# The level-1 block of a triangular inverse: masked from PSUM, or from a copy in SBUF

## The reference, cut to what matters

```
def step(s, inp):                      # s: one 64x64 state per head and direction
    r_t, w_t, k_t, v_t, aa_t, bb_t = inp
    sa = einsum('dbhij,dbhj->dbhi', s, aa_t)
    s = s * w_t[..., None, :] + sa[..., :, None] * bb_t[..., None, :] + v_t[..., :, None] * k_t[..., None, :]
    y_t = einsum('dbhij,dbhj->dbhi', s, r_t)
    return s, y_t
state, ys = lax.scan(step, state0, xs)  # 256 context tokens, then 256 latent tokens, 2 directions, 8 heads
```

## Time and profile before

| what | value |
|---|---|
| median of 3 runs | 2276.77 us (2275.12 to 2277.88) |
| profiled execution | 2275.12 us, its span 2273.3 us |
| PE busy | 2195.0 us, 97% of the span |
| DVE busy | 691.6 us, 30% |
| ACT busy | 355.3 us, 16% |
| POOL busy | 96.9 us, 4% |
| mean granted PE clock | 0.989 of full speed |

### The profile page before, as it was taken

How to read it: one execution, slowest core, us unless ns; L and a number is a source line. 1 busy time by engine, 2 the same in 40 slices (tenths; PEclk the granted TensorE clock), 3 DMA queues, 4 the chain that set the end, 5 groups by cost and what they waited for, 6 DMA issues and landing times.

```text
span 2273.3 us, 34037 instructions
## 1 busy us (share of the span) xinstructions
PE 2195.0 (97%) x15007; PEld 1350.1 (59%) x15008; DVE 691.6 (30%) x1187; ACT 355.3 (16%) x771; POOL 96.9 (4%) x114
## 2 busy tenths in 40 slices
PE   7999999999999998999998999999999999999997
PEld 6667786888677775478887553344344444444432
DVE  0000100621275424347777531211111211211113
ACT  1000200240100012243343111000001110100000
POOL 1000000000100000202212000000000000000000
PEclk9999999999999999999999989999999999999999
DMA  9655444244678961000001589999999999999996
GB/s 318 189 155 184 170 139 148 84 139 152 213 250 275 285 213 56 1 3 3 3 22 50 210 344 426 425 426 423 426 424 427 426 422 419 421 424 426 426 426 273
DMA packets 199428, 582.16 MB, mean 256 GB/s; under 512 B 9620, under 2 KB 153808, under 8 KB 166384
## 3 DMA queue, kind: packets, MB, share of 16 engines
q1 hardware_dynamic: 194656, 564.70, 64.4%
q0 software_dynamic: 4208, 13.27, 1.6%
q10 hardware_dynamic: 416, 1.99, 0.2%
HBM read 576.52 MB, written 3.42 MB: 255 GB/s over the span
## 4 chain that ended last, share of the span: by engine, by line
PE 91%; DVE 5%; DMA 2%; ACT 1%; issue 1%; SPq 1%; DVEq 0%
PE ps L2581 22%; PE ps L610 13%; PE ps L2593 10%; PE ps L671 8%; PE ps L619 7%; PE ps L1340 5%; PE ps L2560 3%; PE ps L2608 3%; PE ps L802 2%; PE ps L775 2%; PE ps L1670 2%; PE ps L1690 1%; PE ps L1772 1%; PE ps L976 1%; DMA arena<-in_w 1%; PE ps L1687 1%
## 5 line engine op out<-in xcount | busy, mean ns | idle before, releaser
L2581 PE MATMUL ps<-ring,const 128*64 128x512 f32 (+1 forms) x1536 | 474.5, 597 | 0.0
L2581 PEld LDWEIGHTS ps<-ring,const 128*64 128x64 f32 (+1 forms) x1536 | 160.8, 144 | 306.5 <-issue 306.2
L610 PE MATMUL ps<-arena,ring 128*128 128x256 f32 x1408 | 314.1, 381 | 1.8 <-DMA ring<-in_ffn_w_down 1.8
L610 PEld LDWEIGHTS ps<-arena,ring 128*128 128x128 f32 x1408 | 265.2, 190 | 46.5 <-issue 11.0
L2581 PE MATMUL ps<-arena,const 128*64 128x512 f32 (+1 forms) x512 | 225.7, 593 | 0.0
L2593 PE MATMUL ps<-ring,const 128*64 128x512 f32 (+1 forms) x768 | 190.1, 594 | 0.0
L671 PE MATMUL ps<-arena,ring 128*128 128x256 f32 x800 | 173.1, 379 | 0.0
L2805 DVE TENSOR_SCALAR arena<-ps 128x1024 f32<-128x1024 f32 x18 | 22.0, 1225 | 469.2 <-PE ps L2581 469.2
L671 PEld LDWEIGHTS ps<-arena,ring 128*128 128x128 f32 x800 | 151.9, 190 | 20.7
L619 PE MATMUL ps<-ring,arena 128*128 128x512 f32 x352 | 157.6, 592 | 0.0
L2593 PEld LDWEIGHTS ps<-ring,const 128*64 128x64 f32 (+1 forms) x768 | 65.1, 143 | 111.7 <-issue 110.2
(11 more groups left out here) (484 smaller groups left out, 2400.8 us busy)
## 6 DMA issues: line engine op xcount, KB each, us to landing
ring<-in_w SPq DMA_DIRECT2D x96, 2048.0 KB, 17.7
ring<-in_w SPq DMA_DIRECT2D x96, 1024.0 KB, 15.2
arena<-in_w SPq DMA_DIRECT2D x32, 2048.0 KB, 18.6
ring<-in_w_in SPq DMA_DIRECT2D x26, 1536.0 KB, 6.9
arena<-in_w SPq DMA_DIRECT2D x32, 1024.0 KB, 17.5
ring<-in_w_ada SPq DMA_DIRECT2D x16, 1536.0 KB, 9.2
ring<-in_ffn_w_gate SPq DMA_DIRECT2D x44, 512.0 KB, 3.9
ring<-in_ffn_w_up SPq DMA_DIRECT2D x44, 512.0 KB, 5.4
```

What stands on the lines that cost most here:

```text
L610: ins = pe.matmul(ps[:, j % 2, half * S:(half + 1) * S], s[:, col0:col0 + P], uT[:, k, :], start=(k == 0), stop=(k == KD - 1))
L2581: ins = pe.matmul(ps[a * n:(a + 1) * n, q, :], xsT[:, k, a * n:(a + 1) * n], chunk(chunks[a])[:, q * 512:(q + 1) * 512], start=False, stop ...
```

## The change

DVE no longer takes `near` out of PSUM. The 2x2 blocks for `TI[:, 1]` are now taken from `MbT`, which the first two mask instructions have just written to SBUF, under a mask `lev1` that is built like those of the other levels. This instruction stands behind `first` instead of ahead of it. PE's second products wait for the two `Mb` counts instead of `near`. POOL's wait for `T0` at the second level is gone. The constant table loses two masks of 64 columns and gains one.

```
@@ -145,8 +145,7 @@
         after = (ic > jc) if d == 0 else (ic < jc)
         cols[f"first{d}"] = after & ((ic // 2) == (jc // 2))
-        cols[f"near{d}"] = before & ((ic // 2) == (jc // 2))
-    for b in (2, 4, 8, 16, 32):
+    for b in (1, 2, 4, 8, 16, 32):
         cols[f"lev{b}"] = ((ic // (2 * b)) == (jc // (2 * b))) & ((ic // b) != (jc // b))
@@ -1642,7 +1641,7 @@
         def products_end_pe(pe, v):
-            pe.wait_ge(*at("near", v + 1))
+            pe.wait_ge(*at("Mb", 2 * v + 2))
             with_rows(pe, v, KT).then_inc(*up("Mk_mm"))
@@ -1974,8 +1973,6 @@
                     if n >= 2:
                         p.wait_ge(*at("Z_mm", 2 * (n - 1)))
-                    if l == 1:
-                        p.wait_ge(*at("T0", v + 1))
                     p.tensor_tensor(ME[:, (n % 2) * RH:(n % 2 + 1) * RH, :], MbT[v % 2][:, 0, :, :],
@@ -2024,6 +2021,7 @@
+            every = [P, RH, HN]
@@ -2031,13 +2029,11 @@
             for b in range(2):
                 masked(MbT[q], b).then_inc(*up("Mb"))
-            def inner(dst, b, name):
-                return d.tensor_tensor(dst.rearrange("p (b q) n -> p b q n", b=2), halves(b, 0).rearrange("p b (q n) -> p b q n", n=HN),
-                                k_(name).unsqueeze(1).unsqueeze(1).to_broadcast([P, 2, HP, HN]), ALU.mult)
-            inner(TI[q][:, 1, :, :], 0, f"near{dr}").then_inc(*up("near"))
             d.wait_ge(*at("Ti_mm", v + 1))
-            inner(TI[q][:, 0, :, :], 2, f"first{dr}").then_inc(*up("dve_own"))
-            d.wait_ge(*now("near"))
+            d.tensor_tensor(TI[q][:, 0, :, :].rearrange("p (b q) n -> p b q n", b=2), halves(2, 0).rearrange("p b (q n) -> p b q n", n=HN),
+                            k_(f"first{dr}").unsqueeze(1).unsqueeze(1).to_broadcast([P, 2, HP, HN]), ALU.mult).then_inc(*up("dve_own"))
+            d.wait_ge(*now("Mb"))
+            d.tensor_tensor(TI[q][:, 1, :, :], MbT[q][:, 0, :, :], k_("lev1").unsqueeze(1).to_broadcast(every), ALU.mult).then_inc(*up("dve_own"))
             d.wait_ge(*now("dve_own"))
             d.tensor_tensor(TI[q], TI[q], id64.unsqueeze(1).unsqueeze(1).to_broadcast([P, 2, RH, HN]), ALU.add).then_inc(*up("T0"))
```

## The result

The changed kernel takes **2297.08 us** (median of 6 runs, 2293.89 to 2299.93), the kernel before 2276.66 us (6 runs): ratio 1.0094, 95% interval 1.0084 to 1.0103. It is 20.4 us slower. The direction was forecast, the size was not: the forecast was 12.8 us, and 2297.08 lies above the range, which ended at 2294.0.

A forecast was written before the change was run, and what follows sets the result against it. PE was taken as the bound, busy 97% of the span, with DVE mattering where PE waits for `T0`. Late `T0`, 8 x 1.60 = 12.8 us, on the 2276.77 us median gave 2289.6 us; range 2283.5 to 2294.0.

The forecast's parts named there:

- `T0` on the path in all 8 visits: PE before L1670: any delay of `T0` delays the end equally, 8 times; bringing it forward gains at most 4.9 us.
- L2036 ends 0.55 after POOL, POOL 1.13 after it, the addition 1.09 after that; 1.60 a visit: DVE meeting POOL's level masks: these three delays make `T0` 1.60 us late per visit, 12.8 us in all.
- The alternation: DVE and POOL take turns by whole instructions, so POOL's second mask goes ahead of the identity addition; 1.60 us a visit.
- the addition goes first: Rival: the identity addition on DVE runs ahead of POOL's second mask; 0.71 us a visit, 2282.5 us; chance 0.05.
- So the visits bear such gaps: PE before L1670: idle may grow from 0.5 to 2.1 us, about 3.1 in visit 7, without the clock falling.
- the rival of the clock: PE's clock falls behind the longer gaps: 1.2 us a visit, 9.6 in all, on top; about 2299 us; chance 0.03.
- The row at 0.70 in the same group: Earlier trace, stretch 1262 to 1266: granted clock 0.70 with PE busy 2.57 of 4 us; basis for the clock rival's price.
- visit 7 as the first: By the skill's rule on idle gaps, visit 7, with the longest gap, would be first to lose PE's higher clock.
- Everything hidden: Side effects on PE, POOL and DVE hidden behind other waits, each taken as worth 0.
- PE's earlier second products: They may start 0.6 us earlier, when `Mb` is complete; worth 0, at most 0.6 us.
- POOL's earlier second mask: Ready about 1.4 us before PE could use it, its result not needed until the second level; worth 0.
- the order on DVE: `first` stands where `near` stood, five instructions of the same widths before `T0`; taken as 0, at most 0.1 us a visit.

The follow-up runs named there:

- The run with the gap filled: The changed kernel with two useless 512-column matmuls behind PE's second products in each visit; 2290.80 us, ratio 1.0059 to the kernel before.
- POOL's freedom alone: The kernel before without POOL's wait for `T0` at the second level, `near` still from PSUM; 2280.44 us, ratio 1.0011.

## Why the prediction was wrong

- **`T0` on the path in all 8 visits**: right. There were 18.1 us of waits against 17 to 18 forecast.
- **L2036 ends 0.55 after POOL, POOL 1.13 after it, the addition 1.09 after that; 1.60 a visit**: right: 0.54, 1.13, 1.08, and 1.58 in visit 1. The run with the gap filled measures the whole term: 13.5 us where 12.8 were forecast.
- **The alternation**: right for this kernel, but read too widely. It is not that a waiting POOL goes ahead of any DVE instruction. Who is queued at the moment of release goes. The rival "the addition goes first" had its real condition there, 0.05 us away.
- **The step that failed** is "So the visits bear such gaps", in the rival of the clock. It got 0.03 and was the case. It rested on two stretches of the earlier trace rows with a clock of 1.00 and little work on PE. One holds a single wait of 2.58 us, the other two, of 1.56 and 0.92, all in one execution. The runs show in its place that the clock may or may not fall behind a gap of one length, as in visits 1 and 2 of the changed kernel, and that the falls made some 7.8 of the 20.4 us. The wait of 2.58 us itself shows it. It stands at L1728 in visit 6, and the kernel with `first` repeated once has it 0.02 us shorter. Here are the stretches behind it, the kernel before first:

```profile
1209.85 0.62 PE L1728 MATMUL ps<-arena,ring 64*64 64x64 f32 x26 [2.58 <-issue]
1209.00:1217.00 8.00, 6.08 (x214) 5.94 (x215) 3.54 (x6) 0.77 (x2) 1.27 (x1) 1.00 0.39 139
...
1215.90 0.62 PE L1728 MATMUL ps<-arena,ring 64*64 64x64 f32 x26 [2.56 <-issue]
1215.00:1223.00 8.00, 7.10 (x204) 7.10 (x205) 1.98 (x3) 0.77 (x2) 1.27 (x1) 0.79 0.40 139
```

Eight of the 13 profiles have PE waiting there, for 2.29 to 2.85 us. The clock fell right behind it in three and stayed at 1.00 in five. Two rows at 1.00 said that such a gap can pass, not that eight will. The row at 0.70 in the same group, with more work on PE, was the warning. The price set on the rival, 1.2 us a visit and 9.6 in all, came near partly by luck: too little for one fall (1.1 to 1.6 us), and eight falls where there were five. The medians give 7.8. 2299 was forecast for it, 2297.1 came.
- The sentence of the Trainium skill there (TensorE: Matmul & The Clock Gate, section "Why this matters for your kernels"), that one idle gap between bursts can put the clock back to the lower level, holds here, though not each time. The gaps that it warns of are longer than those of 2.1 to 2.2 us behind which the clock fell in visits 1, 3, 4 and 6, and the measurement decides. The prediction named visit 7 as the first and said that the trace had no such gap in the visits to try the rule on. It had one, the 2.58 us above.
- **Everything hidden**: PE's earlier second products, POOL's earlier second mask and the order on DVE were each set at 0. The exchange of the order measured 0. For POOL's freedom alone 3.1 us are open. PE's earlier second products were not tried alone. A slip of no weight stands there: by the prediction's own times POOL's second mask is ready 1.1 us ahead of `T0` (1044.99 and 1046.08), not about 1.4.

## What to carry to other kernels

When an edit lengthens a wait of PE that recurs, price the wait and then the matmuls behind it: here gaps grown from 0.5 to 2.1 us cost 12.6 us of waiting and 7.8 us of slower matmuls, and filling them with useless work gave 6.3 back. Before a DVE operand is moved from PSUM to SBUF, lay POOL's instructions beside it, and ask at each end of one who is already queued. A chain can be shortened by signalling the half that the reader needs first, if the other half is kept clear of everything that waits.

## What the runs showed of the hardware

- DVE instructions with both operands in SBUF and POOL's masks exclude each other for whole instructions, and in these rows the one that is waiting goes next: an addition queued 0.05 us before POOL's mask ended went ahead of the next mask; one issued 0.04 us after DVE's own instruction had ended went behind it, a difference of 1.1 us per visit.
- The clock fell behind gaps of 2.08 us in visits 1 and 3 and not behind 2.07 and 2.09 us in visits 0 and 2 of one execution. 1.73 and 1.74 us at the same place in two kernels went both ways, and so did 2.58 and 2.56 us at L1728. Behind eight gaps of 1.22 to 1.64 us, with `first` repeated once, only 0.6 us were left over, which is inside the interval.
- The 31 executions of the changed kernel spread over 8.4 us and follow their mean clock: 2293.5 us at 0.988, 2301.9 us at 0.983.
